# Two products a chunk instead of three for the narrow projections, with a folding product behind them

## What is computed

```python
def deltanet_mixer(h, w_in, ...):
    proj = h @ w_in                                        # 1024 x (4*1024 + 16)
    b_logit = proj[..., 4 * kd:4 * kd + DN_HEADS]          # 8 columns
    a_in = proj[..., 4 * kd + DN_HEADS:]                   # 8 columns
    ...
def moe_ffn(h, router_w, router_b, ...):
    logits = (t @ router_w) + router_b                     # 8 columns
    top_vals, top_idx = lax.top_k(logits, TOP_K)
    ...
def second_block(x, mem, ...):
    proj = jnp.einsum('bsd,de->bse', h, w_in[l])
    ... f_logit ...                                        # 8 columns of w_in
    log_f = jax.nn.log_sigmoid(f_logit + b_forget[l])
```

## Time and profile before

| | |
|---|---|
| median of 3 runs | 1866.09 us (1865.03 to 1867.91) |
| the profiled execution | 1865.44 us |
| its span in the trace | 1863.4 us, granted TensorE clock 0.999 |
| PE busy | 1835.2 us (98%) |
| PE weight loads busy | 1522.8 us (82%) |
| DVE busy | 1435.4 us (77%) |
| ACT busy | 1234.7 us (66%) |
| POOL busy | 91.7 us (5%) |

### The profile page before, as it was taken

The page is one execution under the profiler, slowest core; times in us unless marked ns, Lnnn a source line. Parts: engine busy times, 40 slices in busy tenths (PEclk is TensorE's granted clock), DMA queues, the critical chain, the costliest instruction groups (busy, mean ns, idle before and its releaser), DMA issues.

```text
span 1863.4 us, 26626 instructions
## 1 busy us (share of the span) xinstructions
PE 1835.2 (98%) x9714; PEld 1522.8 (82%) x9714; DVE 1435.4 (77%) x1246; ACT 1234.7 (66%) x1107; POOL 91.7 (5%) x130
## 2 busy tenths in 40 slices
PE   9999999889999999999999999999999999999998
PEld 7888887787788888888888888888877788888887
DVE  5654567777988988989889898888997777776554
ACT  6544467465778778787787777877767468745452
POOL 0100011120100000000000000000401100000000
PEclk9999999999999999999999999999999999999999
DMA  8974544015999999999999999999995333445551
GB/s 317 386 279 154 206 157 158 25 71 237 387 400 376 392 381 389 358 380 396 362 401 368 372 409 364 386 376 370 382 384 203 141 131 112 162 179 186 191 188 68
DMA packets 76780, 521.10 MB, mean 280 GB/s; under 512 B 8224, under 2 KB 8480, under 8 KB 17568
## 3 DMA queue, kind: packets, MB, share of 16 engines
q1 hardware_dynamic: 72368, 503.27, 69.9%
q0 software_dynamic: 4192, 16.25, 2.2%
q10 hardware_dynamic: 144, 0.52, 0.1%
HBM read 501.14 MB, written 18.87 MB: 279 GB/s over the span
## 4 chain that ended last, share of the span: by engine, by line
PE 76%; DVE 3%; issue 1%; ACT 1%; POOL 0%; DVEq 0%; ACTq 0%; POOLq 0%
PE bank L931 16%; PE bank L926 16%; PE bank L927 16%; PE bank L556 7%; PE bank L563 7%; PE bank L557 7%; PE bank L948 1%; DVE w_lo L2423 1%; PE bank L628 1%; PE bank L749 1%; PE bank L605 0%; PE bank L1199 0%; DVE w_lo L2068 0%; PE bank L976 0%; PE bank L759 0%
## 5 line engine op out<-in xcount | busy, mean ns | idle before, releaser
L2423 DVE TENSOR_TENSOR w_lo<-raw,w_hi 128x2048 fp32r<-128x2048 f32 x336 | 762.1, 2289 | 101.6 <-ACT w_hi L1639 98.0
L1639 ACT ACTIVATE w_hi<-raw 128x2048 fp32r<-128x2048 f32 x336 | 643.2, 1919 | 146.4 <-PE bank L931 145.4
L2068 DVE TENSOR_TENSOR w_lo<-raw,w_hi 128x2048 fp32r<-128x2048 f32 (+2 forms) x137 | 298.2, 2184 | 127.1 <-ACT w_hi L1415 125.1
L1415 ACT ACTIVATE w_hi<-raw 128x2048 fp32r<-128x2048 f32 (+2 forms) x137 | 250.4, 1830 | 169.2 <-PE bank L563 161.4
L926 PE MATMUL bank<-w_hi,xT 128*128 128x512 f32 x896 | 353.7, 395 | 0.8 <-issue 0.8
L927 PE MATMUL bank<-w_hi,xT 128*128 128x512 f32 x896 | 349.4, 390 | 0.0
L556 PE MATMUL bank<-w_hi,xT 128*128 128x512 f32 (+1 forms) x752 | 294.1, 393 | 1.3 <-ACT w_hi L1415 1.0
L557 PE MATMUL bank<-w_hi,xT 128*128 128x512 f32 (+1 forms) x752 | 288.9, 386 | 0.0
L931 PE MATMUL bank<-w_lo,xT 128*128 128x512 f32 x896 | 240.4, 390 | 2.7 <-DVE w_lo L2423 2.6
L931 PEld LDWEIGHTS bank<-w_lo,xT 128*128 128x128 f32 x896 | 167.9, 188 | 39.5 <-DVE w_lo L2423 4.3
L926 PEld LDWEIGHTS bank<-w_hi,xT 128*128 128x128 f32 x896 | 168.3, 188 | 34.8 <-issue 1.0
(11 more groups left out here) (473 smaller groups left out, 1820.6 us busy)
## 6 DMA issues: line engine op xcount, KB each, us to landing
raw<-in_experts_dram SPq DMA_DIRECT2D x336, 1024.0 KB, 7.0
raw<-in_tiles_dram SPq DMA_DIRECT2D x124, 1024.0 KB, 4.8
rows_in<-zeros POOLq DMA_DIRECT2D x1, 6144.0 KB, 32.7
raw<-in_tiles_dram SPq DMA_DIRECT2D x11, 512.0 KB, 4.1
rows_out<-zeros POOLq DMA_DIRECT2D x1, 5632.0 KB, 54.8
item_rows<-rows_in SPq DMA_DIRECT2D x7, 512.0 KB, 7.2
rows_out<-y_s SPq DMA_DIRECT2D x7, 512.0 KB, 3.5
row<-in_rows_dram SPq DMA_DIRECT2D x1, 1040.0 KB, 12.9
```

The lines of the kernel that those rows point to most:

```text
L1415: nc.scalar.activation(w_hi[:, i % SPL, 0:kc * w], raw[:, i % DENSE, 0:kc * w], ACT.Copy)\
L1639: nc.scalar.activation(w_hi[:, w_slot(j), :], raw[:, raw_slot(j), :], ACT.Copy).then_inc(m_hi, 1)
L2068: nc.vector.tensor_tensor(w_lo[:, i % SPL, 0:kc * w], raw[:, i % DENSE, 0:kc * w], w_hi[:, i % SPL, 0:kc * w], ALU.subtract).then_inc(spli ...
L2423: nc.vector.tensor_tensor(w_lo[:, s, :], raw[:, raw_slot(j), :], w_hi[:, s, :], ALU.subtract).then_inc(m_lo, 1)
```

## The change

High and low columns of the narrow weights lie in one buffer, `narrow_both`, in groups of eight: eight high columns, then the eight low ones that belong to them, so that a projection of n columns is one stationary operand of 2n. Each chunk takes two products, with `xT2` and with `xT1`, into 2n partitions of the bank. (The product of low weights with low activations, which was not made before, is now among them.) DVE copies 2n partitions to `narrow_T`. The transposes become products with a constant matrix `fold` of ones, which turn the result and add the two halves in one step. The constants grow by 16 columns, from 1439 to 1455.

```diff
+                  ("fold", 16)):
...
+    c16 = np.arange(16)[None, :]
+    put("fold", (i < 32) & (i % 8 == c16 % 8) & (i // 16 == c16 // 8))
...
-        narrow_hi = sb("narrow_hi", [P, KD, 32], FR)
-        narrow_lo = sb("narrow_lo", [P, KD, 32], FR)
+        narrow_both = sb("narrow_both", [P, KD, 64], FR)
+        narrow_hi, narrow_lo = (narrow_both[:, :, :].rearrange("p k (a b c) -> p k a b c", a=4, b=2)[:, :, :, b, :]
+                                for b in range(2))
...
-                n = cols.stop - cols.start
+                n = 2 * (cols.stop - cols.start)
                 for k in chunks:
-                    w1, w2 = narrow_hi[:, k, cols], narrow_lo[:, k, cols]
-                    nc.tensor.matmul(b[0:n, 0:S], w2, xT1[:, k, :], start=k == 0, stop=False)
-                    nc.tensor.matmul(b[0:n, 0:S], w1, xT2[:, k, :], start=False, stop=False)
-                    last = nc.tensor.matmul(b[0:n, 0:S], w1, xT1[:, k, :], start=False, stop=k == KD - 1)
+                    w = narrow_both[:, k, 2 * cols.start:2 * cols.stop]
+                    nc.tensor.matmul(b[0:n, 0:S], w, xT2[:, k, :], start=k == 0, stop=False)
+                    last = nc.tensor.matmul(b[0:n, 0:S], w, xT1[:, k, :], start=False, stop=k == KD - 1)
...
-                    last = nc.tensor.transpose(b[:, tt * n:tt * n + n], narrow_T[0:n, tt * P:tt * P + P],
-                                               ident[0:n, 0:n])
+                    last = nc.tensor.matmul(b[:, tt * n:tt * n + n], narrow_T[0:2 * n, tt * P:tt * P + P],
+                                            C("fold")[0:2 * n, 0:n], start=True, stop=True)
...
-            tell(nc.scalar.activation(narrow_hi[:, :, :], narrow[:, :, :], ACT.Copy), narrow_split)
+            tell(nc.scalar.activation(narrow_hi, narrow[:, :, :].rearrange("p k (a c) -> p k a c", a=4), ACT.Copy), narrow_split)
...
-                tell(nc.vector.tensor_copy(narrow_T[0:n, :], batch((name, "T"))[0:n, 0:S]), tp_free["D"])
+                tell(nc.vector.tensor_copy(narrow_T[0:2 * n, :], batch((name, "T"))[0:2 * n, 0:S]), tp_free["D"])
...
-            nc.vector.tensor_tensor(narrow_lo[:, :, :], narrow[:, :, :], narrow_hi[:, :, :], ALU.subtract)\
+            nc.vector.tensor_tensor(narrow_lo, narrow[:, :, :].rearrange("p k (a c) -> p k a c", a=4), narrow_hi, ALU.subtract)\
```

More of the change, by code:

```diff
@@ L54 @@
 for _name, _n in (("ident", P), ("ones", P), ("upto", P), ("before", P), ("from_", P), ("future", P),
-                  ("iota", P), ("levels", HALF * len(LEVELS)), ("ident2", HALF), ("jlt", NE * NE), ("one_at", 4 * HEADS - 1)):
+                  ("iota", P), ("levels", HALF * len(LEVELS)), ("ident2", HALF), ("jlt", NE * NE), ("one_at", 4 * HEADS - 1),
+                  ("fold", 16)):
     CONST_AT[_name] = (_at, _at + _n)
@@ L2358, in experts @@
                 gained_half(1)
-                tell(nc.vector.tensor_copy(narrow_T[0:NE, :], batch(("router", "T"))[0:NE, 0:S]), tp_free["D"])
+                tell(nc.vector.tensor_copy(narrow_T[0:2 * NE, :], batch(("router", "T"))[0:2 * NE, 0:S]), tp_free["D"])
                 b = batch("router")
@@ L2615, in headed @@
                         if name == "fxk":
-                            tell(nc.vector.tensor_copy(narrow_T[0:8, :], batch(("forget", "T"))[0:8, 0:S]), tp_free["D"])
+                            tell(nc.vector.tensor_copy(narrow_T[0:16, :], batch(("forget", "T"))[0:16, 0:S]), tp_free["D"])
                         head_scale(name)
```

## The result

The changed kernel takes 1902.61 us (median of 4 runs, 1902.07 to 1904.82) against 1865.59 us before (1865.03 to 1867.91). The ratio is 1.0196, 95% interval 1.0183 to 1.0208: 37 us slower, where I forecast 0.94 us less. The span grows from 1863.4 to 1900.8 us, and the granted clock is 0.997 in the mean where it was 0.999: those 0.2% are at most 4 of the 37 us, so the clock is not the reason.

A forecast was written before the change was run, and what follows sets the result against it. PE's own sequence of matmuls was taken to set the time almost everywhere. 1865.44 - 0.94 - 0.02 = 1864.5 us for the profiled execution, so a median of 1865.1 us, range 1862.7 to 1867.8.

The forecast's parts named there:

- the five named cases: The forecast 0.58, all savings counting 0.10, none counting 0.12, a wider load setting the pace 0.06, moved issue stalls 0.14.
- The sum over the edits: Whole kernel: gains of 0.94, 0.02 and 0 us at the three edited places, 1864.5 us for the profiled execution.
- Place 1: Narrow products from 247.09 us: eight fewer save 0.94 us, the added fold is covered by a later wait; gain 0.94 us.
- the rival of the wider load: At 0.19 us a product, loading more stationary columns sets the narrow products' pace: 1866.7 us; chance 0.06.
- The fold: Two float32 products replace two transposes at each place: 0.41 us instead of 0.22, adding 0.19 us on PE.
- Its cover: PE's 0.67 us wait for DVE at 289.71 us absorbs the fold's 0.19 us and shrinks to 0.48.
- None of it counts: Rival: DVE and ACT alone set 256 to 290 us, so the 0.94 us is lost: 1866.1 to 1866.5 us; chance 0.12.
- Place 2: Narrow products in two halves, second from 445.32 us: PE's wait for DVE's split grows 0.37 to 0.83 us; gain 0.02 us.
- Place 3: Where PE, after turning the result, waits 0.86 us for DVE's scaled heads: savings and fold vanish in that wait; gain 0.
- all of it counts: Rival: waits at the second and third places move with PE, so 2.8 us go at all three: 1863.9 us; chance 0.10.
- The issue stalls: Rival: PE's two unexplained stalls in the delta rule, 1.6 us in all, shift: 1863.9 or 1866.3 us; chance 0.14.
- The sign that I had named for it: The `L563` tile behind the routing products, at 453.67 us before, starts 0.9 to 1.0 us earlier, the span ending likewise.

The follow-up runs named there:

- i_same_layout: The whole change, with the matrix of ones in its own buffer behind the work area, so all other buffers keep their old addresses: 1866.76 us, ratio 1.0000.
- j_change_256: The whole change with 192 empty bytes ahead of the narrow weights, a move of 256 bytes against the kernel before: 1866.49 us, ratio 1.0000.
- j_change_512: The whole change with 448 empty bytes ahead of the narrow weights, a move of 512 bytes against the kernel before: 1864.45 us, ratio 0.9990.
- d_all_shift: The kernel before with 64 empty bytes ahead of `raw`, so weights, xT and hid all move by 64 bytes: 1867.38 us, ratio 1.0001.

## Why the prediction was wrong

**The step that failed** is the last case in the chances: "0.06 for slower, for what no row shows, such as buffers that now lie 64 bytes further on", together with "the constants grow by 16 columns in 1439, a hundredth of one load at the very start; zero as well". I counted the constants' transfer and priced the move of everything behind them at nothing. It was worth 5.2 ns on each of some 7,100 products that the change doesn't touch. None of the named rivals has it, and the range, 1862.7 to 1867.8, reached only as far as they did. The trace before held no second layout to read the price from. (The chances also add up to 1.11: the five named cases make 1.00, and the 0.05 and 0.06 come on top.)

**The sum over the edits** holds once the distances are back: 1866.76, 1866.49 and 1864.45 us stand against 1866.39 us of the kernel before on the same chip, and the forecast of 0.96 us less, a ratio of 0.9995, lies in all three intervals. Term by term, in the trace of `i_same_layout`:

Place 1. The narrow products:

```profile
246.50 0.28 PE L642 MATMUL bank<-xT,narrow_both 128*32 128x256 f32 x1
...
248.33 0.40 PE L561 MATMUL bank<-w_hi,xT 128*128 128x512 f32 x1
...
253.89 0.61 PE L653 MATMUL bank<-fold_m,narrow_T 32*128 32x16 f32 x4
...
254.43 1.09 PE L673 MATMUL bank<-cst,xn 128*128 128x128 f32 x8
...
288.08 1.13 PE L695 MATMUL bank<-cst,A 128*128 128x128 f32 x8 [0.34 <-DVE kT L2154]
```

They take 1.83 us, 0.114 each, so 32 stationary columns go at the old pace and the rival of the wider load falls. The fold is the term that was mis-sized: 0.54 us, not 0.41, so it adds 0.32 us and not 0.19. Its cover holds: the wait behind it shrinks from 0.67 us to 0.34, where I said 0.48. From the first narrow product to the end of that wait the trace before has 289.71 - 247.09 = 42.62 us, this one 41.58: 1.04 us gained, 0.94 forecast. It is not the luck of one execution: by the starts of the same DVE instructions `i_same_layout`, `j_change_256` and `j_change_512` gain 1.04, 1.05 and 1.03 us on the kernel before between 201 and 297 us, and `d_all_shift`, which has none of the change, gains 0.02. "None of it counts" falls with it.

Place 2. The wait for the second half grew, on the weight loads, from 0.37 us to the forecast 0.83:

```profile
445.99 0.09 PEld L642 LDWEIGHTS bank<-xT,narrow_both 128*16 128x16 f32 x1 [0.83 <-DVE xT L2105]
...
447.42 0.41 DVE L2364 COPY narrow_T<-bank 16x256 f32<-16x256 f32 x1
447.97 0.52 PEld L653 LDWEIGHTS bank<-fold_m,narrow_T 16*128 16x128 f32 x4 [0.36 <-DVE narrow_T L2364]
```

DVE's copy starts without waiting for PE now, as forecast. From the second half's start to the tile behind the routing products are 8.23 us (445.99 to 454.22) against 8.35 before: 0.12 us gained where I said 0.02.

Place 3. The wait for the scaled heads grew from 0.86 us to 1.44, not to 1.7: the eight products saved add 0.9 to it, and the fold, as long as at place 1, takes 0.32 off.

```profile
1458.46 0.61 PE L653 MATMUL bank<-fold_m,narrow_T 16*128 16x8 f32 x4
1459.23 1.23 DVE L2580 TENSOR_TENSOR xn<-xn,small 128x1024 f32<-128x1024 f32 x1 [3.92 <-POOL small L1947]
1460.51 1.36 PE L1026 MATMUL bank<-cst,xn 128*128 128x128 f32 x8 [1.44 <-DVE xn L2580]
```

DVE's scaling and PE's turning both start 2.12 us later than in the earlier trace rows, a lag that this trace has had from 500 us on: nothing gained there, as forecast, and "all of it counts" falls. The issue stalls show no move that goes with the change: 1.5 us in two waits against 1.6, the same 1.5 in `j_change_512`, and 2.3 in `j_change_256`.

**That lag** is the one thing the sum could not hold. The sign that I had named for it fails: the tile behind the routing products, which was to start 0.9 to 1.0 us before 453.67, starts 0.55 us behind it.

```profile
454.22 1.63 PE L568 MATMUL bank<-w_lo,memT 128*128 128x512 f32 x6
```

The 1.04 us are gone again by then, because single executions differ by more. Windows of the kernel before, of the unchanged kernel at other addresses (`d_all_shift`) and of `i_same_layout`:

```profile
370.00:385.00 15.00, 12.14 (x435) 11.03 (x431) 10.54 (x13) 9.45 (x23) 1.04 (x2) 0.97 0.02 4
465.00:475.00 10.00, 8.11 (x36) 6.37 (x35) 9.62 (x15) 9.46 (x7) 6.65 (x3) 1.00 0.73 244
```

```profile
370.00:385.00 15.00, 11.97 (x407) 10.62 (x403) 10.00 (x13) 8.82 (x23) 1.04 (x2) 0.91 0.01 3
465.00:475.00 10.00, 8.14 (x29) 6.22 (x28) 9.52 (x19) 8.68 (x6) 6.15 (x3) 0.83 0.70 252
```

```profile
370.00:385.00 15.00, 12.54 (x345) 11.20 (x337) 9.16 (x11) 8.48 (x22) 1.04 (x2) 0.81 0.02 3
465.00:475.00 10.00, 8.14 (x30) 6.21 (x29) 9.52 (x17) 8.52 (x6) 6.41 (x3) 0.83 0.75 250
```

In the delta rule's small matmuls and behind the 1.9 us wait at the start of the experts the granted clock (third column from the right) falls further in one execution than in another, in the unchanged kernel too: a mean of 0.83 from 465 to 475 us there, so part of that window went by at the lower of the two levels, 1.2 instead of 2.4 GHz, and 1.00 in the execution that I had profiled. By the starts of the same DVE instructions, `d_all_shift` falls 2.6 us behind the kernel before between 355 and 484 us, without any change, `i_same_layout` 3.8 us, `j_change_512` 2.8 and `j_change_256` 2.4. That hides a gain of 1 us: of the three layouts that keep the distance two show no difference, and the interval of the third ends just under 1, at 0.9999.

## What to carry to other kernels

An edit that lengthens a buffer moves all that is allocated behind it; where PE sets the time, as here, look at the distance between each stationary and moving operand modulo 256 bytes before and after, or put new buffers at the end. When every product of a kind slows from the first on, at full clock and with no new wait, suspect the layout, and test it with the old kernel and some empty bytes ahead of its buffers. Undo the layout before judging the edit itself.

## What the runs showed of the hardware

- The same product of 128 by 512 takes 226.7 to 234.2 ns by the distance of its operands alone; 0, 240, 256, 512 and 1024 bytes off the old distance are free, 64 bytes cost 6.6 ns.
- A shorter weight load was no gain here: with 32 stationary columns the loads take 108 ns instead of 188, and the products come every 231.7 ns instead of 226.7.
- A float32 product with 8 or 16 moving columns and 128 stationary ones takes 0.27 us in the fold (16 or 32 rows), where the five of the earlier trace rows (128 rows) have 0.206 each. Why is not shown.
